# Gate and up projections as seven block products, with the low weight parts taken from PSUM copies

## Chip, cores and metric

One core of one Trainium2 chip. The metric is the device time of the whole kernel in microseconds, the median of several runs; lower is better. Weights and activations are float32.

## What is computed

Three transformer layers over 512 tokens of width 1024: one with a sparse attention and a recurrent branch, then two with differential attention and a pooling branch. The part that matters here stands at the end of each layer (D is 1024, the hidden width 2816):

```python
x = x + merged @ w_out
h2 = rmsnorm(x, norm2_g)
x = x + (silu(h2 @ w_gate) * (h2 @ w_up)) @ w_down
```

## The kernel before

Everything is kept transposed: features on the 128 partitions, the 512 tokens along the columns, so that a [1024, 512] activation is 8 tiles of 128x512 (`xT`). Every float32 matmul is made of three in the fast float32 mode: each operand is split into a high part (rounded) and a low part (the rest), and high x high, high x low and low x high are summed in PSUM. A weight chunk is one column of eight 128x128 tiles (`chunk`, L1058): 24 matmuls of 512 columns for 8 tiles. SyncE loads chunks into a ring of four raw buffers `wraw` (`load`, L530); an engine splits a chunk into a slot (high part first, then low part), and the counters `w_hi` and `w_lo` tell how many chunks are split, `used` how many TensorE has read. `drained` counts result tiles taken out of PSUM.

The end of a layer is the `tail`, written once per engine (L522, L875, L1953, L2664): 8 chunks of w_out; 44 chunks of gate and up in turn; 24 chunks of down, three for each of 8 output tiles (8, 8 and 6 weight tiles). The PSUM banks are `psA` (2), `psS` (2), `psT` (3) and `psO` (1). In the tail:

- GpSimd splits all weights but w_out's first two chunks (`split`, L735: L743 makes the high part, L745 the low part), into two slots, for down into three. It may write a slot when the chunk two (or three) before has been used.
- VectorE adds each w_out tile to `xT` (L1472), makes its low part (L1474) and sums the squares for the norm (L1479); ScalarE makes the high part (L2347) and the square (L2348). After the eighth tile TensorE sums over the partitions (`norm`, L1092) behind the first gate chunk, and ScalarE and VectorE turn that into the scale `c_rs` (L2337 to L2341, L1484 to L1487).
- VectorE drains each gate and up chunk with the scale (L1461), multiplies the two (L1966) and makes the low part (L1969); ScalarE makes the silu (L2672) and the high part (L2674). The result `hid` [2, 22 tiles, 512] is what down reads.
- VectorE adds down's tiles to `xT` and prepares the next layer's operands, as for w_out.

Each engine works its list in order, and only the counters tie the lists together. The matmuls of the second and third layer's query, key and value stage (`rows`, L1307) have 256 columns each.

## Time and profile before

| | us |
|---|---|
| median of 3 runs | 2600.02 (2596.5 to 2602.19) |
| span of the profiled execution | 2597.4 |
| TensorE busy | 2538.9 |
| VectorE busy | 1200.3 |
| ScalarE busy | 834.5 |
| GpSimd busy | 1159.6 |

The page's busy table gives the share of the span for which each engine works; the chain tells which work ended last, step by step, and how much of the span it carries. Rows of a group "line engine op, out<-in" show busy time, the mean duration of one instruction in ns, and the idle time before them with who ended it. Rows of a timeline show start, duration, engine, line and shape, and in brackets the idle time before and who ended it; matmuls one after another are merged into one row with their count.

### The profile page before, as it was taken

The numbers are of one execution on the slowest core, as the hardware profiler recorded it, in microseconds if no ns is written. First come the engines' busy times: TensorE is split into PE (matmuls) and PEld (weight loads), VectorE is DVE, ScalarE is ACT, GpSimd is POOL, SyncE is SP. The second block draws the span as 40 slices with busy tenths as digits, with TensorE's granted clock in tenths as the row PEclk, the third lists the DMA queues.
The fourth block names the chain that finished last, engine by engine and source line by source line (L and its number), as shares of the span: only waits on it lengthen the run. The fifth ranks groups of instructions, "written<-read, shape, count | busy, mean of one in ns | idle before, by whom it ended". The sixth has DMA issues, their size and how long they took to land.

```text
span 2597.4 us, 37755 instructions
## 1 busy us (share of the span) xinstructions
PE 2538.9 (98%) x12947; PEld 2154.6 (83%) x12947; DVE 1200.3 (46%) x2275; ACT 834.5 (32%) x1473; POOL 1159.6 (45%) x586
## 2 busy tenths in 40 slices
PE   7999999999999999999999999999999999999998
PEld 6789988887888888899988888888899888888887
DVE  6567776664432221277775322211577765322211
ACT  4456655663211110144444211100244443211101
POOL 4335530000377788600000777788300002877885
PEclk8989989999999999999999999999999999999999
DMA  7321113332333333322232233333222222333332
GB/s 156 105 49 33 38 37 89 98 90 81 93 92 97 97 101 97 93 70 70 70 94 83 87 93 96 96 103 94 87 82 70 70 82 81 97 97 97 95 95 77
DMA packets 422189, 222.88 MB, mean 86 GB/s; under 512 B 59504, under 2 KB 420268, under 8 KB 422060
## 3 DMA queue, kind: packets, MB, share of 16 engines
q1 hardware_dynamic: 419100, 218.03, 29.6%
q10 hardware_dynamic: 2960, 3.22, 0.4%
q8 instruction: 71, 1.16, 0.2%
q14 instruction: 58, 0.48, 0.1%
HBM read 212.86 MB, written 2.10 MB: 83 GB/s over the span
## 4 chain that ended last, share of the span: by engine, by line
PE 88%; DVE 7%; ACT 3%; issue 2%; DMA 0%; DVEq 0%; ACTq 0%; POOL 0%
PE psA L1066 48%; PE psB L1089 13%; PE psA L1089 10%; PE psA L1322 5%; PE psB L1322 4%; PE psO L967 3%; PE psB L948 1%; PE psB L924 1%; DVE b L2013 1%; DVE b L2161 1%; DVE b L2053 0%; DVE b L1688 0%; DVE b L2034 0%; PE psO L1362 0%; DVE b L1672 0%
## 5 line engine op out<-in xcount | busy, mean ns | idle before, releaser
L1066 PE MATMUL psA<-b,b 128*128 128x512 f32 x5616 | 1288.0, 391 | 3.8 <-DVE b L1461 1.8
L1066 PEld LDWEIGHTS psA<-b,b 128*128 128x128 f32 x5616 | 1055.3, 188 | 234.5 <-issue 8.6
L743 POOL TENSOR_TENSOR b<-b,b 128x1024 fp32r<-128x1024 f32 x239 | 453.0, 1895 | 1202.5 <-PE psA L1066 1042.3
L745 POOL TENSOR_TENSOR b<-b,b 128x1024 fp32r<-128x1024 f32 x239 | 593.9, 2485 | 18.8
L1089 PE MATMUL psB<-b,b 128*128 128x512 f32 (+4 forms) x1626 | 367.3, 384 | 7.7 <-DVE b L1897 4.5
L1089 PEld LDWEIGHTS psB<-b,b 128*128 128x128 f32 (+2 forms) x1626 | 299.1, 195 | 68.1 <-DVE b L1897 4.9
L1089 PE MATMUL psA<-b,b 128*128 128x512 f32 x1356 | 324.4, 394 | 0.0
L1461 DVE SCALAR_TENSOR_TENSOR b<-psA,b 128x512 f32<-128x512 f32 x152 | 104.6, 690 | 461.6 <-PE psA L1066 457.7
L1089 PEld LDWEIGHTS psA<-b,b 128*128 128x128 f32 x1356 | 252.6, 188 | 54.4 <-issue 1.0
L1472 DVE TENSOR_TENSOR b<-b,psA 128x512 f32 x48 | 33.0, 688 | 337.9 <-PE psA L1066 337.9
L2347 ACT ACTIVATE b<-b,b (+1 forms) x56 | 40.6, 724 | 441.1 <-DVE b L1472 434.5
L2674 ACT ACTIVATE b<-psB 128x512 f32 x66 | 39.5, 598 | 370.3 <-DVE psB L1966 370.3
L1322 PE MATMUL psA<-b,b 128*128 128x256 f32 x1152 | 148.7, 288 | 2.2 <-DVE b L1472 2.2
L1322 PE MATMUL psB<-b,b 128*128 128x256 f32 x1152 | 147.8, 288 | 0.5 <-DVE b L2013 0.5
L1322 PEld LDWEIGHTS psA<-b,b 128*128 128x128 f32 x1152 | 143.7, 194 | 5.6 <-issue 4.9
L1322 PEld LDWEIGHTS psB<-b,b 128*128 128x128 f32 x1152 | 143.2, 194 | 2.7 <-issue 2.3
L2013 DVE TENSOR_TENSOR b<-b,b 128x1024 fp32r<-128x1024 f32 x102 | 124.4, 1220 | 13.7 <-ACT b L2689 13.7
L2689 ACT ACTIVATE b<-b 128x1024 fp32r<-128x1024 f32 x102 | 106.3, 1058 | 55.0 <-PE psA L1089 30.6
L2672 ACT ACTIVATE psB<-b 128x512 f32<-128x512 f32 x66 | 39.7, 602 | 251.9 <-DVE b L1461 251.9
L967 PE MATMUL psO<-b,b 128*128 128x128 f32 x640 | 83.3, 287 | 4.8 <-ACT b L2464 2.5
L967 PEld LDWEIGHTS psO<-b,b 128*128 128x128 f32 x640 | 79.5, 202 | 8.1 <-DVE b L1735 3.5
L2457 ACT ACTIVATE b<-b,b 128x512 f32<-128x512 f32 (+3 forms) x128 | 70.3, 551 | 45.1 <-DVE b L1681 45.1
(271 smaller groups left out, 2177.2 us busy)
## 6 DMA issues: line engine op xcount, KB each, us to landing
b<-in_w_in SPq DMA_DIRECT2D x296, 256.0 KB, 3.0
b<-in_w_ffn_in SPq DMA_DIRECT2D x176, 256.0 KB, 3.1
b<-in_w_ffn_out SPq DMA_DIRECT2D x64, 256.0 KB, 3.0
b<-in_w_out SPq DMA_DIRECT2D x48, 256.0 KB, 3.0
b<-in_w_gate SPq DMA_DIRECT2D x44, 256.0 KB, 3.1
b<-in_w_up SPq DMA_DIRECT2D x44, 256.0 KB, 3.2
b<-in_w_down SPq DMA_DIRECT2D x32, 256.0 KB, 3.0
b<-in_w_ffn_out SPq DMA_DIRECT2D x32, 192.0 KB, 2.6
```

The costliest lines, as they stand in the source:

```text
L743: nc.gpsimd.tensor_tensor(w[:, 0], wraw[:, s], ones[:, 0:1].broadcast_to([P, KT * P]), ALU.mult).then_inc(w_hi.sem, 1)
L745: nc.gpsimd.tensor_tensor(w[:, 1], wraw[:, s], hi_f(w[:, 0]), ALU.subtract).then_inc(w_lo.sem, 1)
L967: i = mm(psO[:, qt * P:(qt + 1) * P], PT[:, h, at:at + P], vtok[:, br, kt, n // 4, hd, :, :].rearrange("p h d -> p (h d)"), start=h == 0 a ...
L1066: i = mm(dst, w[:, wh, kt * P:(kt + 1) * P], rhs(xh, kt), start=first and kt == 0 and n == 0, stop=last and kt == kts - 1 and n == 2)
L1089: i = mm(dst, lh(x), rh(y), start=start and n == 0, stop=stop and n == 2, skip_group_check=skip)
L1322: i = mm(ring(t + q // 2)[:, q % 2 * V2:(q % 2 + 1) * V2], xg[:, xh, kt, q * P:(q + 1) * P], w[:, wh, k * V2:(k + 1) * V2], start=kt == 0 ...
L1461: v.scalar_tensor_tensor(dst, psA[:, s % 2, :], -0.5, c_rs[:, :], ALU.mult, ALU.mult).then_inc(drained.sem, 1)
L2013: v.tensor_tensor(w[:, 1], wraw[:, c % RAW], hi_f(w[:, 0]), ALU.subtract).then_inc(w_lo.sem, 1)
L2347: ac(flat(xg)[:, 0, bass.ds(m * T, T)], x, ACT.Copy, scale=gain).then_inc(res_act.sem, 1)
L2457: ac(pq, pq, ACT.Exp, bias=st[:, o + qt:o + 1 + qt], scale=-1.0, accum_out=st[:, o + 8 + qt:o + 9 + qt]).then_inc(ue_act.sem, 1)
L2672: ac(psS[:, 0, :], fg[:, :], ACT.Silu).then_inc(ff_act.sem, 1)
L2689: ac(w[:, 0], wraw[:, c % RAW], ACT.Copy).then_inc(w_hi.sem, 1)
```

## The change

Gate and up of two hidden tiles each (a "quad": 256 hidden columns of gate, 256 of up) were 4 chunks, 96 matmuls of 512 columns. Seen as blocks, the weights are 2x2 (gate or up; even or odd input tiles) and the activations 2x2 (even or odd input tiles; first or second 256 tokens). Now Winograd's form of Strassen's scheme takes seven block products in place of eight: S1 = A21+A22, S2 = S1-A11, S3 = A11-A21, S4 = A12-S2 of the weights (A11 gate even, A12 gate odd, A21 up even, A22 up odd), and t1 to t4 of the activations. One product is 24 matmuls of 256 columns (`product`); there are 11 quads, 77 products a layer, in unrolled code.

- **Loads.** SyncE loads a quad's four raw blocks with four transfers of 512 KB into one of two buffers (`wraw` and the new `wraw2`), the down weights of the first four chunks ahead of time.
- **Sums of weights.** GpSimd makes S1, S2, S4, S3 (`sum_low`, `sum_high`), splits off the low parts of A12 and A22 (`low`), and adds the first and the fifth product. It no longer splits w_out's chunks; down's it still does, from when the last product's weights are ready.
- **Splits.** ScalarE makes the high parts of all seven (`hi`), and for A11, S1, S2, S4 and S3 copies the source to two PSUM banks (`psS`), from which VectorE makes the low part (`lo`). Each slot is one of three. ScalarE and VectorE split w_out's chunks 2 to 7 as well (`out_hi`, `out_lo`, two instructions over 1024 columns a chunk).
- **Operands.** While w_out runs, ScalarE and VectorE make t1 to t4 and the high and low parts for all of them from the tiles of `xT` (`even_operands`, `odd_operands`, `odd_lo`). The norm's matmul comes behind the second product.
- **Results.** VectorE sums the products in PSUM (`middle_sum`, `gate_high`, `gate_low`, `up`: seven instructions a quad of 512 columns), ScalarE makes one silu of 1024 columns a quad, VectorE two products into `hid_raw`. The up half isn't scaled by the norm; down's result is, before it is added.
- **Hidden parts.** `hid` lies over `hid_raw`, the operands and the raw weights, so its parts are made at the end, 11 times over 1024 columns each: ScalarE the high part (`hidden_hi`), VectorE the low part (`hidden_lo`). TensorE's first down column waits for them pair by pair.

The diff, cut to its core:

```diff
-            stage(c0 + 8, 2 * FT, lambda i, s: (up if s % 2 else gate)(i * 2 * P + (s // 2) * P))
-            stage(c0 + 8 + 2 * FT, 24, lambda i, s: down(s % 3 * KT, i * 4 * P + (s // 3) * P), per=12)
...
+            for q in range(QUADS):
+                if q == 0:
+                    mixed()
+                elif q == 1:
+                    sp.wait_ge(w_lo.sem, w_lo.at(c1 - 1))
+                else:
+                    sp.wait_ge(w_lo.sem, w_lo.at(c1 + place_of(q - 2, S3)))
+                settled(sp)
+                for x in range(2):
+                    for b in range(2):
+                        dst = quad_raw(q)[:, 2 * x + b, :].rearrange("p (j n) -> p j n", n=2 * P)
+                        sp.dma_start(dst, quad(x, b, q)).then_inc(quad_in[q % 2], 16)
...
+            sp.wait_ge(w_lo.sem, w_lo.at(c1 + place_of(QUADS - 2, S3)))
+            settled(sp)
+            for s in range(24):
+                load(c2 + s, s % RAW, down(s % 3 * KT, s // 3 * P), free=s < RAW)
...
+                def sum_low(q):
+                    pool.wait_ge(quad_in[q % 2], loads(q))
+                    settled(pool)
+                    if q:
+                        pool.wait_ge(w_lo.sem, w_lo.at(c + place_of(q - 1, S4)))
+                        settled(pool)
+                    raw = quad_raw(q)
+                    nc.gpsimd.tensor_tensor(sum1[:, :], raw[:, 2, :], raw[:, 3, :], ALU.add).then_inc(sa_pool.sem, 1)
+                    pool.wait_ge(sa_pool.sem, sa_pool.at(g + q, "s1"))
+                    settled(pool)
+                    nc.gpsimd.tensor_tensor(sum2[:, :], sum1[:, :], raw[:, 0, :], ALU.subtract).then_inc(sa_pool.sem, 1)
+                def sum_high(q):
+                    raw = quad_raw(q)
+                    pool.wait_ge(sa_pool.sem, sa_pool.at(g + q, "s2"))
+                    settled(pool)
+                    pool.wait_ge(w_lo.sem, w_lo.at(c + place_of(q, S1)))
+                    settled(pool)
+                    nc.gpsimd.tensor_tensor(sum1[:, :], raw[:, 1, :], sum2[:, :], ALU.subtract).then_inc(sa_pool.sem, 1)
+                    nc.gpsimd.tensor_tensor(raw[:, 2, :], raw[:, 0, :], raw[:, 2, :], ALU.subtract).then_inc(sa_pool.sem, 1)
...
+                    if q == 0:
+                        low(q, A12)
+                    sum_high(q)
+                    if q:
+                        low(q, A12)
+                    low(q, A22)
+                    pool.wait_ge(fs_act.sem, fs_act.at(g + q, "fifth"))
+                    settled(pool)
+                    nc.gpsimd.tensor_tensor(fifth_product, fifth_product, first_product, ALU.add).then_inc(ff_pool.sem, 1)
             def down_splits(c, r):
...
+                pool.wait_ge(w_hi.sem, w_hi.at(c - 1))
+                settled(pool)
+                pool.wait_ge(w_lo.sem, w_lo.at(c - 1))
+                settled(pool)
                 with pool.Fori(0, 2) as i:
...
+                            i = nc.tensor.matmul(banks[x][:, p * half_t:(p + 1) * half_t], w[:, wh, at:at + P], rhs[x][:, xh, j, :],
+                                                 start=first and j == 0 and p == 0 and m == 0,
+                                                 stop=last and j == KT // 2 - 1 and p == 1 and m == 2, skip_group_check=True)
+                i.then_inc(used.sem, 1)
...
+                    if x == A11 and q:
+                        pe.wait_ge(fs_dve.sem, fs_dve.at(g + (q - 1), "g1"))
+                    elif x == A11:
+                        pe.wait_ge(drained.sem, drained.at(t0 + 6))
...
+                        if q == 0:
+                            norm(k, n + 7)
+                            pe.wait_ge(xo_dve.sem, xo_dve.at(x0 + 3, "lo_low"))
+                        pe.wait_ge(fs_act.sem, fs_act.at(g + q, "first"))
+                    elif x == A22 and q:
...
+                        if kt % 2 == 0:
+                            pe.wait_ge(fl_dve.sem, fl_dve.at(g + (q * KT + kt) // 2))
...
+                def even_operands(j):
+                    dve.wait_ge(res_act.sem, res_act.at(n + 2 * j, "hi"))
+                    v.tensor_tensor(even2[:, half_t:T], even2[:, T:T + half_t], even2[:, 0:half_t], ALU.subtract).then_inc(xo_dve.sem, 1)
+                    dve.wait_ge(xo_act.sem, xo_act.at(x0 + j, "hi_even"))
+                    dve.wait_ge(xo_dve.sem, xo_dve.at(x0 + j, "t1"))
+                    v.tensor_tensor(xe[:, 1, 0:2, j, :], even2[:, 0:T].rearrange("p (u t) -> p u t", u=2), hi_f(xe[:, 0, 0:2, j, :]), ALU.subtract).then_inc(res_dve.sem, 1)
+                def odd_operands(j):
+                    dve.wait_ge(res_act.sem, res_act.at(n + 2 * j + 1, "hi"))
+                    v.tensor_tensor(odd_high[:, half_t:T], odd_high[:, 0:half_t], even2[:, half_t:T], ALU.subtract).then_inc(xo_dve.sem, 1)
+                    dve.wait_ge(xo_dve.sem, xo_dve.at(x0 + j, "t2"))
+                    dve.wait_ge(xo_act.sem, xo_act.at(x0 + j, "low"))
+                    v.tensor_tensor(odd_high[:, T:T + half_t], odd_high[:, half_t:T], odd_low, ALU.subtract).then_inc(xo_dve.sem, 1)
+                    v.tensor_tensor(odd_high[:, T + half_t:2 * T], odd_high[:, 0:half_t], even2[:, T:T + half_t], ALU.subtract).then_inc(xo_dve.sem, 1)
+                    dve.wait_ge(xo_act.sem, xo_act.at(x0 + j, "hi_low"))
+                    v.tensor_tensor(xe[:, 1, 2, j, :], odd_low, hi_f(xe[:, 0, 2, j, :]), ALU.subtract).then_inc(xo_dve.sem, 1)
+                def odd_lo(j):
+                    dve.wait_ge(xo_act.sem, xo_act.at(x0 + j))
+                    dve.wait_ge(xo_dve.sem, xo_dve.at(x0 + j, "t3"))
+                    v.tensor_tensor(other[:, 1, :, j, :], odd_high.rearrange("p (u t) -> p u t", u=4), hi_f(other[:, 0, :, j, :]), ALU.subtract).then_inc(res_dve.sem, 1)
...
+                    w = quad_slot(at)
+                    v.tensor_tensor(w[:, 1], psS[:, :, :].rearrange("p b t -> p (b t)"), hi_f(w[:, 0]), ALU.subtract).then_inc(w_lo.sem, 1)
...
+                def up(q):
+                    dve.wait_ge(used.sem, used.at(c1 + place_of(q, S3)))
+                    step(v.tensor_tensor(n_r0[:, :], psA[:, 1, :], first_product, ALU.add))
+                    own(q, "u3")
+                    step(v.scalar_tensor_tensor(psT[:, 2, :], psT[:, 2, :], -1.0, n_r0[:, :], ALU.mult, ALU.add))
+                    dve.wait_ge(ff_pool.sem, ff_pool.at(g + q))
+                    step(v.tensor_tensor(psA[:, 1, :], psA[:, 1, :], fifth_product, ALU.add))
...
+                def hidden_lo(i):
+                    dve.wait_ge(fh_act.sem, fh_act.at(g + i))
+                    at = slice(2 * i, 2 * i + 2)
+                    v.tensor_tensor(hid[:, 0, at, :], hid_raw[:, at, :], hi_f(hid[:, 1, 2 * i:2 * i + 2, :]), ALU.subtract).then_inc(fl_dve.sem, 1)
...
+                    dve.wait_ge(used.sem, used.at(c2 + (3 * m + 2)))
+                    v.scalar_tensor_tensor(psA[:, s, :], psA[:, s, :], -0.5, c_rs[:, :], ALU.mult, ALU.mult).then_inc(dn_dve.sem, 1)
+                    dve.wait_ge(dn_dve.sem, dn_dve.at(d0 + m))
+                    v.tensor_tensor(xT[:, m, :], xT[:, m, :], psA[:, s, :], ALU.add).then_inc(drained.sem, 1)
...
+                for j in range(KT // 2):
+                    added(2 * j)
+                    for w in out_ahead.get(2 * j, []):
+                        out_lo(w)
+                    even_operands(j)
+                    squares_added(2 * j)
+                    if j == 3:
+                        lo(0, A11)
+                        lo(0, S1)
+                    added(2 * j + 1)
+                    for w in out_ahead.get(2 * j + 1, []):
+                        out_lo(w)
+                    odd_operands(j)
+                    squares_added(2 * j + 1)
+                    odd_lo(j)
+                lo(0, S2)
+                lo(0, S4)
                 norm(k)
...
+                for q in range(1, QUADS):
+                    up(q - 1)
+                    product_high(q - 1)
+                    lo(q, S2)
+                    product_low(q - 1)
+                    lo(q, S4)
+                    middle_sum(q)
+                    gate_high(q)
+                    lo(q, S3)
+                    gate_low(q)
+                    if q < QUADS - 1:
+                        lo(q + 1, A11)
+                        lo(q + 1, S1)
+                q = QUADS - 1
+                for i in range(4):
+                    hidden_lo(i)
+                up(q)
+                product_high(q)
+                product_low(q)
+                for i in range(4, 6):
+                    hidden_lo(i)
+                for i in range(6, QUADS):
+                    hidden_lo(i)
...
+                        return
+                    if x != A11:
+                        act.wait_ge(w_lo.sem, w_lo.at(c1 + place_of(q, {S1: A11, S2: S1, S4: S2, S3: S4}[x])))
+                    elif q:
+                        act.wait_ge(w_lo.sem, w_lo.at(c1 + place_of(q - 1, S3)))
+                    ac(psS[:, :, :].rearrange("p b t -> p (b t)"), src[:, :], ACT.Copy).then_inc(wc_act.sem, 1)
...
+                    if j == 3:
+                        hi(0)
+                        hi(1)
+                        hi(2)
...
+                for q in range(QUADS):
+                    c = SEVEN * q
+                    if q:
+                        hi(c + 2)
+                    first(q)
+                    hi(c + 3)
+                    fifth(q)
+                    hi(c + 4)
+                    if q == 0:
+                        norm(k)
+                        nc.scalar.preload_act_table_set("silu_and_others")
+                    hi(c + 5)
+                    hi(c + 6)
+                    hi(c + 7)
+                    if q == QUADS - 1:
+                        hidden_hi(0)
+                        hidden_hi(1)
+                    hi(c + 8)
+                    silu(q)
+                hidden_hi(2)
+                hidden_hi(3)
+                hidden_hi(4)
+                hidden_hi(5)
+                for i in range(6, QUADS):
+                    hidden_hi(i)
```

## Rows read from the trace of the kernel before

**Rows 1.** The page: span, busy time (share) and instructions, chain by engine.

```profile
span 2597.4 us, 37755 instructions
PE 2538.9 (98%) x12947; PEld 2154.6 (83%) x12947; DVE 1200.3 (46%) x2275; ACT 834.5 (32%) x1473; POOL 1159.6 (45%) x586
...
PE 88%; DVE 7%; ACT 3%; issue 2%; DMA 0%; DVEq 0%; ACTq 0%; POOL 0%
```

**Rows 2.** Chain in order of time: start us, us, what, count of matmuls.

```profile
735.18 350.08 PE psA L1066 x1536
...
1203.61 2.92 PE psB L1322 x24
...
1278.49 8.64 PE psB L1322 x72
```

**Rows 3.** Timeline of the gate/up loop, first layer.

```profile
898.72 0.69 DVE L1461 SCALAR_TENSOR_TENSOR b<-psA,b 128x512 f32<-128x512 f32 x1 [4.75 <-PE psA L1066]
...
900.36 0.60 ACT L2674 ACTIVATE b<-psB 128x512 f32 x1 [5.75 <-DVE psB L1966]
900.82 2.40 POOL L745 TENSOR_TENSOR b<-b,b 128x1024 fp32r<-128x1024 f32 x1
901.13 0.69 DVE L1969 TENSOR_TENSOR b<-psB,b 128x512 f32 x1 [0.90 <-ACT b L2674]
...
904.16 0.69 DVE L1461 SCALAR_TENSOR_TENSOR b<-psA,b 128x512 f32<-128x512 f32 x1 [2.33 <-PE psA L1066]
```

**Rows 4.** Groups by line and shape, whole span: busy us, mean ns, idle before.

```profile
L743 POOL TENSOR_TENSOR b<-b,b 128x1024 fp32r<-128x1024 f32 x239 | 453.0, 1895 | 1202.5 <-PE psA L1066 1042.3 <-issue 134.0 <-PE psB L1089 14.1
...
L2013 DVE TENSOR_TENSOR b<-b,b 128x1024 fp32r<-128x1024 f32 x102 | 124.4, 1220 | 13.7 <-ACT b L2689 13.7
L2689 ACT ACTIVATE b<-b 128x1024 fp32r<-128x1024 f32 x102 | 106.3, 1058 | 55.0 <-PE psA L1089 30.6 <-PE psB L1089 18.4 <-PE psA L1322 4.5
```

**Rows 5.** Timeline of VectorE and GpSimd near the kernel's start.

```profile
12.53 1.89 POOL L743 TENSOR_TENSOR b<-b,b 128x1024 fp32r<-128x1024 f32 x1 [12.09 <-DMA b<-in_w_in]
...
13.57 1.40 DVE L1474 SCALAR_TENSOR_TENSOR b<-b,b,b 128x512 fp32r<-128x512 f32 x1
...
14.50 2.68 POOL L745 TENSOR_TENSOR b<-b,b 128x1024 fp32r<-128x1024 f32 x1
...
46.11 2.37 POOL L752 TENSOR_TENSOR b<-b,b 128x1024 fp32r<-128x1024 f32 x1 [5.15 <-ACT b L2403]
46.58 2.44 DVE L1526 TENSOR_TENSOR b<-b,b 128x512 fp32r<-128x512 f32 x1 [1.38 <-ACT b L2380]
```

**Rows 6.** Timeline of the passage from w_out to gate and up.

```profile
717.65 0.69 DVE L1472 TENSOR_TENSOR b<-b,psA 128x512 f32 x1 [2.25 <-PE psA L1066]
...
723.11 0.69 DVE L1472 TENSOR_TENSOR b<-b,psA 128x512 f32 x1 [2.28 <-PE psA L1066]
...
725.26 1.28 ACT L2332 ACT_TABLE_LOAD   x1
...
735.18 10.05 PE L1066 MATMUL psA<-b,b 128*128 128x512 f32 x43 [0.43 <-DVE b L1461]
```

**Rows 7.** Timeline of the last down tiles and the next layer's first matmuls.

```profile
1070.25 0.69 DVE L1472 TENSOR_TENSOR b<-b,psA 128x512 f32 x1 [11.88 <-PE psA L1066]
...
1085.41 0.69 DVE L1472 TENSOR_TENSOR b<-b,psA 128x512 f32 x1 [11.87 <-PE psA L1066]
...
1086.26 6.02 PE L1322 MATMUL psA<-b,b 128*128 128x256 f32 x48 [1.02 <-DVE b L1472]
```

**Rows 8.** Timeline of TensorE after a long wait.

```profile
600.28 12.95 PE L1089 MATMUL psB<-b,b 128*128 128x512 f32 x48 [4.52 <-DVE b L1897]
```

**Rows 9.** Busy time by stretch: PE, PEld, DVE, ACT, POOL, granted clock, DMA share, GB/s.

```profile
600.00:604.00 4.00, 3.72 (x9) 2.94 (x10) 0.22 (x1) 1.88 (x3) 0.00 (x0) 0.57 0.34 102
```

**Rows 10.** DMA issues: count, size of one, median us to landing.

```profile
b<-in_x SPq DMA_DIRECT2D x4, 512.0 KB, 6.1
```

More of the change, by code:

```diff
@@ L857, in _ @@
-            down_splits(C_DN, C_DN // RAW)
+                    for d in range(12):
+                        split(c + i * 12 + d, i * 3 + r + d // RAW, d % RAW, slots2[d % 3], 3)
+            quads(C_GU, 0, lambda q: (q // 2 + 1) * 64)
+            down_splits(C_DN, R_DN // RAW)
             with pool.Fori(0, LAYERS) as l:
-                c0, r0 = l * C_LAYER + C_B2, l * (C_LAYER // RAW) + C_B2 // RAW
+                c0, r0 = l * C_LAYER + C_B2, l * (R_LAYER // RAW) + R_B2 // RAW
                 split(c0, r0, 0, slots2[0], 3)
@@ L1475, in residual @@
                                        ALU.mult, ALU.subtract).then_inc(res_dve.sem, 1)
-                if not add and n:
+                if add is False and n:
                     dve.wait_ge(res_dve.sem, res_dve.at(n - 1))
```

358 lines of the change are left out of this document (265 added, 93 removed).

## The prediction, made before the changed kernel ran

> **What bounds the kernel now.** I read the page's busy table and chain first: TensorE is busy for 98% of the span and carries 88% of the chain that ended last, while VectorE and GpSimd are busy for less than half [rows 1]. So time can only come from fewer or shorter matmuls, and every wait that a change puts on TensorE counts in full. Then the chain in order of time, for the pace of the two matmul shapes: one layer's gate, up and down run 1536 matmuls of 512 columns in 350.08 us with no gap; matmuls of 256 columns run 72 in 8.64 us, 120.0 ns each, and 24 alone in 2.92 us [rows 2]. VectorE's drains in the gate/up loop start every 5.44 us, one chunk of 24 matmuls, 226.7 ns each [rows 3]. Half the columns thus cost 53%: about 13 ns of each matmul don't shrink (2 x 120.0 against 226.7).
>
> **Part A, the products.** Removed per layer: 44 chunks x 5.44 = 239.4 us. Added: 7 x 11 = 77 products of 24 matmuls with 256 columns. At 2.88 us each 221.8, at 2.92 us 224.8; between runs of 72 and single ones I take 2.90, so 223.3. Saving **16.1 us a layer** (14.6 to 17.6), not the eighth (30 us) that the count of columns promises. The code is unrolled; the rows of 256 columns stand in unrolled code too, so its fetching is in that price.
>
> The Trainium skill ("TensorE: Matmul & The Clock Gate", Back-to-back issue gap) gives a matmul's spacing as its columns at 2.4 GHz and 2.5 ns. By it the saving would be an estimated 26 us a layer (44 x 24 at 215.8 ns less 77 x 24 at 109.2). The rows show about 13 ns in place of 2.5 [rows 2, 3], and the sum goes by the rows.
>
> **Do the helpers keep up in the steady quads?** A quad lasts 7 x 2.9 = 20.3 us of TensorE. ScalarE: 12 passes over 1024 columns (7 high parts, 5 PSUM copies; 1.06 each), a silu of 1024 (about 1.1) and 2 copies of 512 (0.60): 15.0 us. VectorE: 5 low parts at 1.22 and 9 sums or products at 0.69: 12.3 us. GpSimd: 6 passes of 2.40 and one of 512 (half, plus overhead, 1.3): 15.7 us [rows 3, 4]. All below 20.3. The tightest chain, with 0.15 us per hand-over, counted from the start of a quad: `up` of the quad before starts at 0.75 (behind the low part of S1), three sums end at 2.95, the product at 3.75, the low part of S2 at 4.95; TensorE wants S2 at 5.8. Its copy then lets S4 be ready at 7.5 (wanted 8.7); GpSimd's A12 is ready at 10.35 (11.6), A22 at 12.85 (14.5). Behind S4's copy, which waits for S2's low part, ScalarE has `fifth` and A12's high part in its queue, and GpSimd's A12 hangs on them: that is in the 10.35. Slack 0.85 us or more: zero cost. If the cover were gone by 1 us per quad, it would be 33 us in all. SyncE issues the loads of 2 MB a quad about 19 us before GpSimd wants them; 512 KB pieces landed within 6.1 us (median) [rows 10].
>
> **The port.** Now where VectorE works on two SBUF operands while GpSimd runs. GpSimd L752 runs 46.11 to 48.48; VectorE's L1526 starts in it at 46.58 and takes 2.44 instead of the 0.69 of such 512-column work, ending 0.54 after it. Between 12.5 and 17.2 they take turns: L1474, 1.40 long, ends 0.55 after L743, and L745 behind it takes 2.68 instead of 2.40 [rows 5]. So one waits for the other's whole instruction. Where one VectorE operand is in PSUM, neither is hurt: L1969 inside L745 takes 0.69, and L745 its 2.40 [rows 3]. The steady quads' VectorE work all has a PSUM operand, so that is where the PSUM copies pay. Not so the operand preparation ahead of quad 0 and the hidden low parts after quad 10. The Trainium skill ("SBUF — State Buffer", Who interferes with whom) says that two SBUF inputs contend with GpSimd's reads as an exclusive lock for a whole instruction; the trace agrees (2.44 for 0.69).
>
> **Part B, the start.** Chunks 6 and 7 of w_out end at 717.5 and 722.95 [rows 6]. While w_out runs, VectorE now also does six weight low parts (1.22) and the operands: a pair of tiles has about 8 us of its own work plus up to two low parts, against 10.9 of TensorE. Quad 0's weights arrive near 702 (SyncE waits for chunk 3's low part at 692.8, then 5 transfers), and GpSimd's two sums put 2.4 us each in VectorE's way. I get tile 6 added at 721.7 instead of 717.7. From there: add 0.7, scale 0.7, difference, high, low of the even operands, squares (to 726.0, hand-overs in), ScalarE's high part of A11 and its copy to 726.65, low part to 728.1: **A11 starts 5.2 us late**, with 0.35 of waiting earlier. Then the low part of S1 at 730.6, tile 7 added 731.3, ScalarE's scalings 732.2. VectorE's t2 waits for GpSimd's A12 (to 733.15), GpSimd's S4 sum follows (735.9), t4, GpSimd's S3 sum (738.6), t3, low, squares, ScalarE's high part, odd low part at 741.5. S1's product ended at 734.0, so **the norm waits 7.5 us**. Behind it ScalarE has first, two high parts with copies, fifth, a high part, a table load (1.28), the roots (2.0), another load and A22's high part, and GpSimd 2.4: A22 at 753.7, **2.9 us late**. Sum 15.9, less what the old start loses (0.43 of wait and the drain's lag, 1.3 in all): **14.6 us** a layer. Without the port in it: idles of 1.8, 2.2 and 2.7, less 1.3: about 5.4. To the other side a long idle also meets a slow clock: after 4.52 us idle the granted clock was 0.57 over the next 4 us, mostly the 1.2 GHz level, and 48 matmuls took 12.95 us instead of the 10.9 of rows 3's pace [rows 8, 9]. Most of that falls into the next wait; 1.7 may be left. Range 5 to 17.
>
> **Part C, the end.** From the start of quad 10: GpSimd's down splits wait for S3's low part, 15.2; each is 1.89 + 2.40 [rows 3, 4]. VectorE's 11 low parts of the hidden pairs (1024 columns, two SBUF operands, 1.22, or 1.1 after a wait) begin at 15.8. TensorE ends S3 at 20.2 and then wants a pair every 1.37 us, the last by about 34. Taking turns: low parts 0 to 3 end at 18.3, 21.8, 24.8, 28.3; then `up` and the products (PSUM, 3.6 us); 4 and 5 end at 33.8 and 36.8; GpSimd's third and fourth split push the last to 45 to 47. TensorE ends the first column at 48 instead of 35.3: 13. If VectorE instead keeps the port through a run, GpSimd's first split is ready at 24.3 instead of 20.7, the second at 36.9 and the third at 41.2, and the column ends at 46.4: 11. The bare port time (11 x 1.15 + 3 x 4.3 from 15.3) gives 41 and 7 us. With something for the clock after the last idle I take **12.5** (7 to 15; 0.3 if the port didn't block).
>
> **Part D.** The down result is scaled before it is added: one more 0.69 and a hand-over on the path to the next stage, where TensorE waits 1.02 for L1472 now [rows 7]: **0.8**. Inside the down loop 15.2 us lie between two drains [rows 7]: nothing.
>
> **The sum.** Per layer -16.1 + 14.6 + 12.5 + 0.8 = +11.8; three layers +35.4. The span of 2597.4 becomes 2632.8; the median of the runs, 2600.0, lies 2.6 above that span [rows 1], so 2635.4.
>
> **The rivals.**
> 1. The port costs next to nothing in these two places (VectorE slips between GpSimd's instructions, or the instructions don't meet). For it: most of VectorE's work here has a PSUM operand. Against it stand both places of [rows 5]. -16.1 + 5.4 + 0.3 + 0.8 = -9.6 a layer: **2571**, faster. It decides by whether L1526's 2.44 repeats in the hidden low parts.
> 2. The port blocks, but the start has the slack that my walk denies it and the end costs its bare port time: -16.1 + 8 + 7 + 0.8 = -0.3: **2599**, no change. For it: my walk chains some thirty steps at 0.15 each.
> 3. The start is mostly covered, the end is not: -16.1 + 7 + 12.5 + 0.8 = +4.2: **2613**.
> 4. The steady chain isn't covered (hand-overs of 0.25 instead of 0.15 eat the 0.85), 1 us a quad on top of the forecast: **2668**. Against: the forecast's chain has few hand-overs between `up` and S2.
> 5. (No case of its own.) The 256-column rate doesn't hold over 20 us at a stretch or the counts don't fall as written: 2.92 and more gives +3.5 us a layer: inside the range.
>
> **How the numbers follow.** Chances: forecast 0.48, rival 1 0.16, rival 2 0.14, rival 3 0.12, rival 4 0.10. A difference of 0.2% (5.2 us) is about what a measurement of this kernel can tell from no change. Faster: rival 1 and half of rival 2's lower side, 0.22. Same: the rest of rival 2 and a little of rival 3, 0.13. Slower: 0.65. The range for 8 in 10 runs from 2566, below rival 1, to 2658; above the worst ends together (starts of 17, ends of 15, products of 2.92: 2655); left out are rival 4 and what no case covers.
>
> **What would show it.** Right: in the gate/up stretch TensorE without idle, groups of 256 columns at 2.88 to 2.92 us per 24; the hidden low parts with a mean of 2 us or more and TensorE waiting for them under L1066 in each of the three layers; a wait of several us ahead of the norm's matmul; split instructions of GpSimd longer than 2.40 in the same places. Wrong: idle inside the quads put down to GpSimd or ScalarE (rival 4), hidden low parts at 1.22 and the down stage starting without a gap (rival 1), or less than 2 us ahead of A11 and of the norm (rivals 2 and 3). If the pace per product is far from 2.9, Part A is wrong.

## The result and the profile after

The changed kernel takes **2615.0 us** (median of 4 runs, 2610.8 to 2620.3) against 2598.8 us of the kernel before in the same runs (2596.5 to 2602.2): a ratio of **1.0062** (95% interval 1.0042 to 1.0081), 16 us slower. The forecast was 35 us slower, 2635. The sign is right and the size is less than half; 2615 lies close to the time of rival 3.

The page of the changed kernel: span, busy table and chain by engine.

```profile
span 2612.9 us, 42576 instructions
...
PE 2503.3 (96%) x15323; PEld 2231.3 (85%) x15323; DVE 1577.8 (60%) x2608; ACT 1289.9 (49%) x1935; POOL 1044.2 (40%) x517
...
PE 81%; DVE 12%; ACT 4%; issue 3%; POOL 0%; DMA 0%; ACTq 0%; DVEq 0%; POOLq 0%
```

TensorE's busy time falls by 35.6 us against [rows 1], and the span grows by 15.5: 51 us of waiting are new. Its share of the chain falls from 88% to 81%, VectorE's rises from 7% to 12%. The waits of the changed kernel name the places (TensorE's longest totals; us, times, longest):

```profile
PE psA L1212 <- DVE b L2201: 23.7, 16, 3.7
PE psO L1240 <- DVE b L2133: 15.4, 3, 5.3
...
PE psA L990 <- DVE b L2147: 10.1, 3, 3.6
```

L1212 is the down projection waiting for the hidden tiles' low parts, L1240 the norm's matmul waiting for the last right operand, L990 the first product of each layer's quads waiting for its weights' low part. There are three layers, and none of these waits lies in the steady quads. TensorE's timeline there (start us, us, count of matmuls; a wait of TensorE would stand in brackets):

```profile
804.35 2.98 PE L990 MATMUL psA<-b,b 128*128 128x256 f32 x24
807.17 3.04 PE L990 MATMUL psB<-b,b 128*128 128x256 f32 x24
810.05 3.04 PE L990 MATMUL psA<-b,b 128*128 128x256 f32 x24
812.93 2.98 PE L990 MATMUL psB<-b,b 128*128 128x256 f32 x24
815.74 5.92 PE L990 MATMUL psA<-b,b 128*128 128x256 f32 x48
821.50 2.98 PE L990 MATMUL psB<-b,b 128*128 128x256 f32 x24
824.31 3.04 PE L990 MATMUL psA<-b,b 128*128 128x256 f32 x24
```

From 804.35 to 824.31 lie seven products, 2.85 us each. From 749.89 to the last product's start at 955.79 there are 72 without a wait: 2.860 us a product, 119.2 ns a matmul.

The start of the quads and the end, same view, with one row of GpSimd (the low part of A22's weights) and the first matmul of A22 behind it at 752.81:

```profile
728.44 4.61 PE L990 MATMUL psA<-b,b 128*128 128x256 f32 x24 [2.98 <-DVE b L2147]
732.89 3.04 PE L990 MATMUL psB<-b,b 128*128 128x256 f32 x24
740.94 2.08 PE L1240 MATMUL psO<-b,b 128*128 128x512 f32 x2 [5.01 <-DVE b L2133]
742.03 8.03 PE L990 MATMUL psA<-b,b 128*128 128x256 f32 x48
...
750.33 2.42 POOL L936 TENSOR_TENSOR b<-b,b 128x1024 fp32r<-128x1024 f32 x1 [12.08 <-ACT b L3000]
...
752.81 0.38 PE L990 MATMUL psB<-b,b 128*128 128x256 f32 x1
...
959.53 3.04 PE L1212 MATMUL psA<-b,b 128*128 128x512 f32 x12 [0.70 <-issue]
...
966.73 1.67 PE L1212 MATMUL psA<-b,b 128*128 128x512 f32 x6 [1.66 <-DVE b L2201]
972.08 5.67 PE L1212 MATMUL psA<-b,b 128*128 128x512 f32 x12 [3.68 <-DVE b L2201]
```

Besides the waits, matmuls behind them are slow: 24 in 4.61 us instead of 3.0, 48 in 8.03 instead of 5.9, 12 in 5.67 instead of 3.0. The granted clock from 726 to 752 is about 0.8, where the kernel before has 1.00 from 728 to 735; from 972 to 978 it is 0.50. Whether slow matmuls cost time depends on what comes next. A22 has no wait in brackets (in the third layer one of 0.26), yet its first matmul starts 0.06 us after GpSimd's low part lands at 752.75, and in the two later layers 0.05 us after it. So TensorE, slowed as it was, arrived there just as its operand did.

What stretches the two chains, in the timeline of VectorE and GpSimd:

```profile
730.85 2.38 POOL L936 TENSOR_TENSOR b<-b,b 128x1024 fp32r<-128x1024 f32 x1 [20.05 <-DVE b L2147]
732.24 1.28 DVE L2122 TENSOR_TENSOR b<-b,b 128x256 f32<-128x256 f32 x1 [0.97 <-ACT b L2976]
733.20 2.58 POOL L926 TENSOR_TENSOR b<-b,b 128x1024 f32<-128x1024 f32 x1
733.55 2.50 DVE L2125 TENSOR_TENSOR b<-b,b 128x256 f32<-128x256 f32 x1
735.73 2.52 POOL L927 TENSOR_TENSOR b<-b 128x1024 f32<-128x1024 f32 x1
735.98 2.56 DVE L2126 TENSOR_TENSOR b<-b,b 128x256 f32<-128x256 f32 x1
...
954.19 1.90 POOL L803 TENSOR_TENSOR b<-b,b 128x1024 fp32r<-128x1024 f32 x1 [1.58 <-DVE b L2147]
954.21 12.46 DVE L2201 TENSOR_TENSOR b<-b,b 128x1024 fp32r<-128x1024 f32 x4
956.17 3.26 POOL L805 TENSOR_TENSOR b<-b,b 128x1024 fp32r<-128x1024 f32 x1
959.39 2.88 POOL L803 TENSOR_TENSOR b<-b,b 128x1024 fp32r<-128x1024 f32 x1
```

Each of VectorE's steps on two SBUF operands ends a fraction of a us after a step of GpSimd, and each GpSimd step behind one of them is longer than it is alone: the pattern of [rows 5], now on TensorE's path. A 256-column difference takes 2.5 us instead of the 0.42 that it takes elsewhere in this trace; the first four hidden low parts take 12.46 us, 3.1 each.

### The profile page after: what moved, and what is told of

Same layout as the page of the kernel before. It is cut to its first block, busy times and chain, and to the rows that moved or that the text cites. A ratio compares the mean times of both kernels' runs of the same rounds, so it can differ in the third digit from the quotient of the medians.

```text
span 2612.9 us, 42576 instructions
## 1 busy us (share of the span) xinstructions
PE 2503.3 (96%) x15323; PEld 2231.3 (85%) x15323; DVE 1577.8 (60%) x2608; ACT 1289.9 (49%) x1935; POOL 1044.2 (40%) x517
## 4 chain that ended last, share of the span: by engine, by line
PE 81%; DVE 12%; ACT 4%; issue 3%; POOL 0%; DMA 0%; ACTq 0%; DVEq 0%; POOLq 0%
PE psA L1212 16%; PE psA L990 14%; PE psB L1235 13%; PE psB L990 10%; PE psA L1235 10%; PE psA L1468 5%; PE psB L1468 4%; DVE b L2201 3%; PE psO L1113 3%; PE psB L1094 2%; PE psB L1070 1%; DVE b L2126 1%; DVE b L2302 1%; DVE b L2450 0%; DVE b L2323 0%
## 5 line engine op out<-in xcount | busy, mean ns | idle before, releaser
L1212 PE MATMUL psA<-b,b 128*128 128x512 f32 x2448 | 577.8, 397 | 28.0 <-DVE b L2201 23.7
L1212 PEld LDWEIGHTS psA<-b,b 128*128 128x128 f32 x2448 | 462.2, 190 | 141.3 <-DVE b L2201 19.9
L915 POOL TENSOR_TENSOR b<-b 128x1024 f32<-128x1024 f32 x33 | 80.0, 2423 | 1030.5 <-DMA b<-in_w_ffn_in 725.1
L990 PE MATMUL psA<-b,b 128*128 128x256 f32 x3168 | 404.0, 286 | 10.1 <-DVE b L2147 10.1
L990 PEld LDWEIGHTS psA<-b,b 128*128 128x128 f32 x3168 | 393.0, 194 | 14.5 <-DVE b L2147 8.0
L1235 PE MATMUL psA<-b,b 128*128 128x512 f32 x1356 | 324.4, 394 | 0.0
L3000 ACT ACTIVATE b<-b 128x1024 fp32r<-128x1024 f32 x231 | 244.2, 1057 | 148.3 <-PE psB L990 79.1
L990 PE MATMUL psB<-b,b 128*128 128x256 f32 x2376 | 299.2, 282 | 0.3 <-POOL b L936 0.3
L1235 PEld LDWEIGHTS psA<-b,b 128*128 128x128 f32 x1356 | 252.5, 188 | 54.4 <-issue 1.0
L990 PEld LDWEIGHTS psB<-b,b 128*128 128x128 f32 x2376 | 290.0, 191 | 0.8 <-POOL b L936 0.7
L2147 DVE TENSOR_TENSOR b<-psB,b 128x1024 fp32r<-128x1024 f32 x165 | 201.8, 1223 | 128.0 <-ACT psB L3007 121.0
L805 POOL TENSOR_TENSOR b<-b,b 128x1024 fp32r<-128x1024 f32 x89 | 235.6, 2647 | 7.0
L936 POOL TENSOR_TENSOR b<-b,b 128x1024 fp32r<-128x1024 f32 x66 | 159.2, 2413 | 166.3 <-ACT b L3000 100.0
L803 POOL TENSOR_TENSOR b<-b,b 128x1024 fp32r<-128x1024 f32 x89 | 178.1, 2001 | 87.8 <-PE psA L1212 36.0
L3007 ACT ACTIVATE psB<-b 128x1024 f32<-128x1024 f32 x165 | 167.2, 1013 | 1.9 <-DVE b L2147 1.5
L1468 PE MATMUL psA<-b,b 128*128 128x256 f32 x1152 | 148.6, 288 | 3.2 <-DVE b L2208 3.2
L1468 PEld LDWEIGHTS psA<-b,b 128*128 128x128 f32 x1152 | 143.6, 194 | 6.7 <-issue 6.0
L1468 PE MATMUL psB<-b,b 128*128 128x256 f32 x1152 | 144.8, 284 | 0.5 <-DVE b L2302 0.5
```

The lines of the kernel that those rows point to most:

```text
L803: nc.gpsimd.tensor_tensor(w[:, 0], wraw[:, s], ones[:, 0:1].broadcast_to([P, KT * P]), ALU.mult).then_inc(w_hi.sem, 1)
L805: nc.gpsimd.tensor_tensor(w[:, 1], wraw[:, s], hi_f(w[:, 0]), ALU.subtract).then_inc(w_lo.sem, 1)
L915: nc.gpsimd.tensor_tensor(sum1[:, :], raw[:, 2, :], raw[:, 3, :], ALU.add).then_inc(sa_pool.sem, 1)
L936: nc.gpsimd.tensor_tensor(w[:, 1], quad_raw(q)[:, {A12: 1, A22: 3}[x]], hi_f(w[:, 0]), ALU.subtract).then_inc(w_lo.sem, 1)
L990: i = nc.tensor.matmul(banks[x][:, p * half_t:(p + 1) * half_t], w[:, wh, at:at + P], rhs[x][:, xh, j, :], start=first and j == 0 and p == ...
L1212: i = mm(dst, w[:, wh, kt * P:(kt + 1) * P], rhs(xh, kt), start=first and kt == 0 and n == 0, stop=last and kt == kts - 1 and n == 2)
```

## The experiments

The theory: the losses at the two ends come from VectorE and GpSimd taking turns at SBUF, each for a whole instruction; the gain is the products' count at the price of a narrow matmul. The rivals: the chains of weights, sums and norm are late by themselves; TensorE's clock is the cost; the narrow matmul costs something else than the forecast says. The first three runs leave out the right values of the steps that they change (the PSUM bank holds other numbers), so they tell the time alone; the others compute the whole result.

**The end without the turns.**

```diff
-  v.tensor_tensor(hid[:, 0, at, :], hid_raw[:, at, :], hi_f(...), ALU.subtract)
+  v.tensor_tensor(hid[:, 0, at, :], psS[:, :, :], hi_f(...), ALU.subtract)
```

> The changed kernel, in which the low part of each pair of hidden tiles (L2201) subtracts from 1024 values of a PSUM bank in place of the tiles in SBUF; so the right low parts of the hidden tiles are left out, and nothing else differs: same count, same shapes, same waits. Port theory: VectorE and GpSimd take turns at the SBUF port between 954 and 984 us of each layer's trace; without the turns VectorE's eleven subtractions take 11 x 1.22 = 13.5 us instead of the 26.9 us (12.46 + 14.41) in the trace, GpSimd's pairs 4.4 us instead of 6.1, and the down projection loses about 1 us instead of 12.0: 3 x 11 = 33 us less than 2615, about 2582. Rival: the end waits for the weights' own split on GpSimd and for the last product's chain, which this edit doesn't touch: 0 to 6 us less, 2609 to 2615.

Measured: 2578.5 us (ratio to the kernel before 0.992, 0.9903 to 0.9938), 36.5 less than the changed kernel. By shape, the hidden low parts of the changed kernel and of this one (count, busy us, mean ns):

```profile
L2201 DVE TENSOR_TENSOR b<-b,b 128x1024 fp32r<-128x1024 f32 x33 | 80.8, 2510 | 0.1
```

```profile
L2201 DVE TENSOR_TENSOR b<-psB,b 128x1024 fp32r<-128x1024 f32 x33 | 38.1, 1214 | 1.6 <-ACT b L3031 1.5
```

TensorE's down projection starts without a gap and takes 121.5 us a layer instead of 133.4, and GpSimd makes the same splits. So where the subtraction reads its second operand is worth 11.9 us a layer; the weights' split was not late by itself.

**The start without the turns.**

```diff
-  v.tensor_tensor(odd_high[:, T:T + half_t], odd_high[:, half_t:T], odd_low, ALU.subtract)
+  v.tensor_tensor(odd_high[:, T:T + half_t], psO[:, 0:half_t], odd_low, ALU.subtract)
...
```

> The changed kernel, in which seven of VectorE's operations on two SBUF operands in the w_out stage (the four differences of the right operands and the three low parts, L2115 to L2133) take one operand from a PSUM bank of the same size; the right differences and low parts are left out, counts, shapes and waits are the same. Port theory of the start: GpSimd's L936, L926 and L927 (2.38, 2.58, 2.52 us) stretch L2122, L2125 and L2126 to 1.28, 2.50 and 2.56 us instead of 0.43 each; without that the wait ahead of the norm's matmul falls from 5.0 to about 1 us, the clock may fall less, and the first product starts as before. 4 to 5 us per layer, 12 to 15 us in all: about 2601. Rival (ScalarE's chain of copies bounds the start as well): no more than 1 us per layer, 2612 to 2615.

Measured: 2593.4 us (0.9979, 0.997 to 0.9989), 21.6 less than the changed kernel, 7.2 a layer, more than the 4 to 5 expected. TensorE at this kernel's start of the quads:

```profile
720.82 3.10 PE L990 MATMUL psA<-b,b 128*128 128x256 f32 x24 [0.31 <-DVE b L2147]
...
728.24 1.13 PE L1240 MATMUL psO<-b,b 128*128 128x512 f32 x2 [1.44 <-DVE b L2133]
728.80 6.28 PE L990 MATMUL psA<-b,b 128*128 128x256 f32 x48
...
740.03 3.11 PE L990 MATMUL psB<-b,b 128*128 128x256 f32 x24 [2.08 <-POOL b L936]
```

The wait ahead of A11 went too, from 2.98 to 0.31: GpSimd's two sums at 705.8 (L915, L918) had stretched VectorE's L2125 and L2126 of the second operand pair to 2.60 and 2.65 us, and no other turns ahead of A11 go with this edit. What I had missed is that turns 20 us ahead of a wait still count when the chain between has no slack: VectorE idles there for 0.2 to 1 us at a time, but mostly for a step of ScalarE on VectorE's own last result. In the later layers the wait ahead of A11 fell from 3.6 to about 1. The granted clock stays at 1.00 from 720 to 752. A wait of 2.08 us now shows at A22, but it is no new loss: A22's low part lands 11.7 us after the norm's matmul starts (728.24 to 739.98), in the changed kernel 11.8 (740.94 to 752.75). There the slow matmuls covered the same delay.

**Both.** 

> The changed kernel with both PSUM substitutions of the earlier runs (hidden low parts at the end, seven operand steps in the w_out stage); the right values of those low parts and differences are left out. It gives the time without the port's turns at either end. If the two losses are apart from each other, the gains add: against 2615, 36.5 us from the end (2615.0 - 2578.5) and 21.6 from the start (2615.0 - 2593.4) make 2557. Rival (one wait hides behind the other): 2565 to 2575.

Measured: 2560.1 us (0.986, 0.9841 to 0.9879), 54.9 less than the changed kernel against 58.1 for the sum, and the runs lie between 2554.7 and 2565.6: within that scatter the two losses add.

**The steady quads without the PSUM copies.**

```diff
-  dve.wait_ge(wc_act.sem, wc_act.at(g + q, ...))
-  v.tensor_tensor(w[:, 1], psS[:, :, :].rearrange("p b t -> p (b t)"), hi_f(w[:, 0]), ALU.subtract)
+  v.tensor_tensor(w[:, 1], src[:, :], hi_f(w[:, 0]), ALU.subtract)    # src: the weights or the sum in SBUF
...
-  ac(psS[:, :, :].rearrange("p b t -> p (b t)"), src[:, :], ACT.Copy).then_inc(wc_act.sem, 1)
```

> The changed kernel without its PSUM copies: VectorE's low parts of the weights (L2147) read the weights and sums in SBUF, and ScalarE's copies (L3007, 1.01 us, five per quad) are gone; the result is whole. Port theory of the steady quads: per quad GpSimd holds the port for six operations of 2.4 us and one of 1.28 (15.8 us), VectorE's five low parts need 5 x 1.22 = 6.1 us of it, together 21.9 us against the 20.03 us that TensorE takes: at least 1.9 us more per quad, 33 quads, 62 us, and more where turns fall badly: 2670 to 2760. Rival (the copies were not needed, ScalarE's relief is worth as much): 2605 to 2620.

Measured: 2693.8 us (1.036, 1.0341 to 1.0378), 79 more than the changed kernel. The low parts of the weights take 2.29 us instead of 1.22, and TensorE waits for them 31 times; this kernel's low parts, its largest wait, and the changed kernel's low parts:

```profile
L2148 DVE TENSOR_TENSOR b<-b,b 128x1024 fp32r<-128x1024 f32 x165 | 378.3, 2293 | 15.8 <-ACT b L3001 12.6 <-POOL b L936 0.7
```

```profile
PE psA L990 <- DVE b L2148: 57.8, 31, 3.0
```

```profile
L2147 DVE TENSOR_TENSOR b<-psB,b 128x1024 fp32r<-128x1024 f32 x165 | 201.8, 1223 | 128.0 <-ACT psB L3007 121.0 <-POOL b L936 6.4 <-issue 0.6
```

GpSimd's two first sums of a quad stretch too (L915 from 2.42 to 3.32 us, L918 from 2.41 to 3.10). So the copies are what lets the quads run without a gap: ScalarE spends 1.01 us on each of 165 and they are worth 79 us.

**The narrow matmul by itself.** In the kernel before:

```diff
-  i = mm(dst, w[:, wh, kt * P:(kt + 1) * P], rhs(xh, kt), ...)
+  for p in range(2):                      # two matmuls of 256 columns
+      at = slice(p * T // 2, (p + 1) * T // 2)
+      i = nc.tensor.matmul(psA[:, s % 2, at], w[:, wh, kt * P:(kt + 1) * P], rhs(xh, kt)[:, at], ...)
```

> The kernel before, in which each 512-column matmul of gate and up is issued as two of 256 columns (48 instead of 24 per chunk, 44 chunks in each of three layers); the result is whole. It measures the price of a narrow matmul by itself. By the changed kernel's steady quads, 20.03 us for 7 x 24 matmuls = 119.2 ns each against 226.7 ns for one of 512: 48 x 0.1192 = 5.72 against 5.44 us per chunk, 0.28 x 132 = 37 us more, about 2636. By the price that the prediction used (2.90 us for 24, 120.8 ns): 5.80 against 5.44, 47 us more, 2646. Rival (half the columns, half the time; the loss of the changed kernel lies elsewhere): 2600.

Measured: 2639.7 us (1.0152, 1.0134 to 1.017), 40.4 more, 0.306 us a chunk: (5.44 + 0.306) / 48 = 119.7 ns. That confirms the pace of the quads (119.2) within 0.5% and lies below the 120.8 ns (2.90 us for 24) that the prediction took.

**Moving the work at the end.** ScalarE and VectorE split the first four chunks of down between the hidden halves; GpSimd starts at chunk 4:

```diff
+  pool.wait_ge(fl_dve.sem, fl_dve.at(g + QUADS - 1))
...
-  with pool.Fori(0, 2) as i:
-      for d in range(12):
-          split(c + i * 12 + d, ...)
+  for d in range(4, 24):
+      split(c + d, r + d // RAW, d % RAW, slots2[d % 3], 3)
```

> The changed kernel, in which the first four chunks of the down projection's weights are split by ScalarE (high) and VectorE (low), woven in between the hidden tiles' halves, and GpSimd starts at chunk 4 once the last hidden low part is done; the result is whole. It tells whether the port can be kept apart by moving work. Port theory: the end loses what VectorE's own queue then costs: from the last quad's gate on it has 11 x 1.22 + 3 x 1.22 + 3.4 us of the last quad's steps = 20.5 us of work from 954.2 on, done at 974.7, where TensorE would want the last pair at 972.5, so 2 to 4 us lost instead of 12.0: 3 x 9 = 27 us less than 2615, about 2588 (2582 to 2594). Rival (the weights' splits were late by themselves, whoever makes them): 2605 to 2615.

Measured: 2583.8 us (0.9949, 0.9933 to 0.9966), 31 less than the changed kernel. One wait is left at the end of each layer:

```profile
956.01 11.26 PE L1215 MATMUL psA<-b,b 128*128 128x512 f32 x48
969.41 20.90 PE L1215 MATMUL psA<-b,b 128*128 128x512 f32 x90 [2.14 <-DVE b L2204]
```

It is 2.14 us (2.02 in the later layers), inside the 2 to 4 that the expectation worked out from VectorE's own queue; down takes 123.7 us a layer instead of 133.4.

**Moving the sums at the start.**

```diff
+  if q == 0:
+      pool.wait_ge(res_dve.sem, res_dve.at(n + 7))     # ahead of L926 and L927
```

> The changed kernel, in which GpSimd's sums of the first quad's S4 and S3 (L926, L927) also wait until the last right operand's low part is made; the result is whole. Port theory: L2125 and L2126 of the last operand pair take 0.43 us instead of 2.50 and 2.56, so the norm's matmul starts 3 to 4 us earlier, if the S4 sum, which is then finished near 739 us instead of 735.8, stays hidden behind S1, A12 and S2: 3 x 3.5 = 10 us less than 2615, 2600 to 2606. Rival (the sum becomes late: S4 waits for it): 2612 to 2618.

Measured: 2611.9 us (1.0052, 1.0036 to 1.0069), only 3.1 less. Neither the theory's size nor the rival's place is right:

```profile
725.25 4.60 PE L993 MATMUL psA<-b,b 128*128 128x256 f32 x24 [3.03 <-DVE b L2150]
...
733.52 1.13 PE L1243 MATMUL psO<-b,b 128*128 128x512 f32 x2 [0.79 <-DVE b L2136]
734.08 6.29 PE L993 MATMUL psA<-b,b 128*128 128x256 f32 x48
...
746.72 4.59 PE L993 MATMUL psB<-b,b 128*128 128x256 f32 x24 [3.47 <-POOL b L939]
```

The norm's wait fell from 5.01 to 0.79 as expected, and 3.47 us show at A22. The norm's matmul starts 4.2 us sooner after w_out's end, but A22's low part only 2.9 (24.4 us after it instead of 27.3), and over the whole layer 1.5 us are left. That low part GpSimd can't make before ScalarE has made the high part, and the high part stands in ScalarE's queue behind the norm's table load and steps. S4, which the rival named, waits for nothing. The next run moves it.

```diff
-  if q == 0:
-      norm(k)
-      nc.scalar.preload_act_table_set("silu_and_others")
   hi(c + 5)                                            # A22's high part
+  if q == 0:
+      norm(k)
+      nc.scalar.preload_act_table_set("silu_and_others")
```

> The kernel with GpSimd's later sums after the operands, and besides A12 ahead of the norm's matmul on TensorE and ScalarE's split of A22's weights ahead of the norm's steps; the result is whole. In the run without the order (2611.9) the wait for the norm's matmul fell from 5.01 to 0.79 us, but TensorE then waited 3.47 us for A22's low part (L936), whose high part stood on ScalarE behind the norm's table load and three steps. Theory (the wait moved there): with the order the 3.5 us come out, less some 1 us for A12's own wait on t3: 3 x 2.5 = 7.5 us less than 2611.9, 2602 to 2606. Rival (GpSimd itself is late with A22 because its sums were put back): 2609 to 2613.

Measured: 2607.4 us (1.0035, 1.0021 to 1.0049), 4.5 less than without the order, less than the 7.5 of the theory and more than the rival allows: A22's wait is gone, but a wait of 1.67 us stands at the first product behind it, for its weights' low part on VectorE, and in the two later layers that wait is 3.41.

**The clock.** In the changed kernel, matmuls without use in the two waits at the start:

```diff
+  for i in range(16):                                  # 32 ahead of the norm's wait
+      nc.tensor.matmul(psO[:, 0:half_t], src[:, 0, 0, 0:P], src[:, 0, 1, 0:half_t], start=True, stop=True)
```

> The changed kernel with matmuls of no use in TensorE's two waits at the start of the quads: 16 of 256 columns (about 1.9 us) ahead of the first product's wait of 2.98 us, 32 (3.8 us) ahead of the norm's wait of 5.01 us; the result is whole. Granted clock between 726 and 752 us is 0.79 to 0.81 in the changed kernel against 1.00 in the same place of the kernel before. Clock theory: TensorE's idle time lowers the clock, which costs 1.6 us in A11 (4.61 against 3.0), 1.0 in the norm's matmul, 1 to 2 us in the 48 matmuls after: 3 to 4 us per layer, so 2604 to 2606. Rival (the stretched matmuls have another cause, or the filler delays the real work): 2614 to 2620.

Measured: 2616.7 us (1.0071, 1.005 to 1.0093): the rival's number. The stretches in question (us; PE, PEld, DVE, ACT and POOL busy; granted clock; DMA share; GB/s), changed kernel, then this one:

```profile
726.00:735.00 9.00, 6.56 (x42) 6.59 (x43) 6.21 (x6) 5.67 (x9) 4.15 (x2) 0.81 0.01 3
735.00:742.00 7.00, 1.99 (x10) 1.27 (x10) 5.69 (x5) 3.43 (x5) 3.25 (x2) 0.79 0.00 0
742.00:752.00 10.00, 10.00 (x68) 9.48 (x67) 5.01 (x6) 9.78 (x11) 1.67 (x1) 0.81 0.00 0
```

```profile
726.00:735.00 9.00, 7.97 (x58) 7.38 (x57) 4.86 (x7) 7.66 (x11) 1.49 (x1) 1.00 0.00 1
735.00:742.00 7.00, 5.93 (x50) 5.72 (x48) 6.96 (x5) 1.33 (x3) 6.01 (x3) 1.00 0.00 0
742.00:752.00 10.00, 8.30 (x53) 7.27 (x54) 5.34 (x7) 9.88 (x13) 0.00 (x0) 0.83 0.01 2
```

The filler holds the clock at its full level, 2.4 GHz, up to 742, and A11 takes 3.11 us again. But the norm's matmul starts 15.7 us after w_out's end, in the changed kernel 15.5: VectorE sets that moment, and A11's slow matmuls lay inside the wait. Behind the norm 2.77 us of idle time were left uncovered and the matmul there took 2.08 us as before; 0.9 us gained in the 48 matmuls after it went into a wait of 0.75 at A22. A lower clock inside a stretch that waits anyway costs nothing. Behind the norm this run didn't remove it, but the traces settle that part too: A22 starts when its low part lands, in this run (755.48, start at 755.53) as in the changed kernel (752.75, 752.81), and GpSimd's low part waits for ScalarE (L3000), not for TensorE. So up to A22 none of the loss is the clock's.

**All moves together.** The kernel v3 has both moves, the new order, and A11's weights one operand pair earlier.

> The changed kernel with the edits of the two runs beside it (the first four chunks of down split by ScalarE and VectorE; the first quad's later sums after the operands), and with a new order at the start of the quads: the weights of the first product are split one operand pair earlier, A12 runs ahead of the norm's matmul, ScalarE splits A22's weights ahead of the norm's steps. The result is whole. Port and order theory: 27 us from the end, 10 us from the sums, and 1 to 3 us per layer from the A11 and norm waits and the clock that falls with them: 2615 - 27 - 10 - 6 = 2572 (2564 to 2582), below the kernel before at 2599. Rival (ends gain, start is bounded by ScalarE's own chain): 2580 to 2588.

Measured: 2575.5 us (0.991, 0.9893 to 0.9927), inside the theory's range. The kernel v4 adds four moves, the first from a line of v3's trace in the second layer: the norm's scale on VectorE, two SBUF operands, met GpSimd's sums for the second quad, and S3 waited (VectorE, then TensorE):

```profile
1486.04 2.94 DVE L1637 SCALAR_TENSOR_TENSOR b<-b,b 128x512 f32<-128x512 f32 x1
...
1491.65 6.20 PE L996 MATMUL psA<-b,b 128*128 128x256 f32 x48 [3.41 <-DVE b L2152]
```

```diff
+  if q == 1:
+      pool.wait_ge(nm_dve.sem, nm_dve.at(k, "scale"))  # ahead of the second quad's sums
...
+  pool.wait_ge(fl_dve.sem, fl_dve.at(g + 8))           # VectorE is now in five steps that read PSUM
+  nc.gpsimd.tensor_tensor(slots2[2][:, 1], wraw[:, 2], hi_f(slots2[2][:, 0]), ALU.subtract)
```

> The kernel of v3_both_ends with four more moves, the result whole: GpSimd's sums for the second quad wait until VectorE has the norm's scale (in layers 2 and 3 L915 and L918 stretched L1637 to 2.94 us and S3 waited 3.41 us); ScalarE loads silu's table after S3's weights; at the end GpSimd makes the low part of chunk 2 while VectorE is in the five steps of the last quad that read PSUM; these five steps stand ahead of pair 9 instead of pair 8. Port theory: start 2 us less in each of layers 2 and 3, end 2.14 us of wait become 1.1 in each of three layers: 4 + 3 = 7 us less than 2575.5, 2566 to 2571. Rival (GpSimd's step beside PSUM reads is not free, or its later sums are late for S1 and S2 of the second quad): 2574 to 2580.

Measured: **2559.1 us** (0.9845, 0.9828 to 0.9861), 16 less than v3 and 9 less than the theory's middle. Between the two traces the three layers give 14.8 of it: 1.8 a layer in the stretch from w_out's end to the last product, 3.1 in down (125.3 to 122.2). The four moves weren't run one by one, so how much each brings is not shown. In its trace the scale takes 0.69 again and S3's wait is 1.18. At the end GpSimd's low part and VectorE's steps run side by side, and neither is stretched:

```profile
1695.84 0.68 DVE L2197 TENSOR_TENSOR b<-psA,b 128x512 f32<-128x512 f32 x1
1696.10 2.40 POOL L966 TENSOR_TENSOR b<-b,b 128x1024 fp32r<-128x1024 f32 x1 [14.90 <-ACT b L3057]
1696.56 0.70 DVE L2199 SCALAR_TENSOR_TENSOR psB<-psB,b 128x512 f32<-128x512 f32 x1
```

Down takes 122.2 us a layer, 0.8 above the run without turns. Per layer, from w_out's end to the last product, the stretch is 226.1 us on average (changed kernel 233.9, v3 227.9). It is 1.5% faster than the kernel before and 2.1% faster than the changed one.

## Why the prediction was half right

Per layer the changed kernel takes, from w_out's start to down's end, 411.0 us (681.18 to 1092.16). In the kernel before, w_out starts at 679.15 and down ends at 1085.24 [rows 7]: 406.1. So 4.9 a layer (5.2 and 5.3 in the later two), and 0.6 behind it; the forecast had 11.8. The mechanism held: the losses came where the forecast put them and by the turns that it named. Two terms of its sum were mis-sized, the price of a product in Part A and the walk up to the norm in Part B.

- **A, the products: forecast -16.1, measured -19.2** (77 x 2.860 = 220.2 against 239.4). The step that failed is "between runs of 72 and single ones I take 2.90". [rows 2] offered 120.0 ns a matmul over a run of 72 and 121.7 over 24 alone. The longest run, 2.88 us a product, would have taken away 1.5 of the error of 3.1 us a layer; that the pace over 72 products is 2.860 no row of before showed. That half the columns cost 53% of the time was right, and it is why the count's eighth didn't come: measured 119.7 ns against 226.7 for twice the columns, 12.7 ns a matmul that don't shrink.
- **B, the start: forecast +14.6, measured about +12.2** (4.9 + 19.2 - 11.9, the last being C). The step that failed is the walk up to the norm's matmul. It put that matmul 18.5 us after w_out's end (A11 5.2 late, two products of 2.9, a wait of 7.5); measured are 15.5, with waits of 2.98 and 5.01 for the same releasers and 1.6 us of slow clock in A11 between them, which the norm's wait would have held otherwise. Already tile 6 was added 2.9 us later than in the kernel before (41.4 against 38.5 us after w_out's start), where the walk had 4.0. "A22 2.9 us late" was nearly right: A22 starts 11.9 us after the norm's matmul, forecast 12.2. It shows as slow matmuls (2.08 and 8.03 us for work of 1.0 and 5.9) in place of a wait. So the clock at nothing, "most of that falls into the next wait", was right as well. The port's part is 7.2 a layer (second run), forecast 14.6 - 5.4 = 9.2; what remains without it is 5.0, forecast 5.4.
- **C, the end: forecast +12.5, measured +11.9** (133.4 against 121.5 in the first run). Mechanism, place and size as forecast: VectorE and GpSimd alternate through the stretch, the hidden low parts average 2.51 us ("2 us or more"), and the last one ends 45.7 us after the last quad's start (938.65 to 984.32), where the walk had 45 to 47. The 12 matmuls at half the clock (5.67 us) end ahead of further waits for low parts.
- **D: forecast +0.8, measured +0.6** (the wait ahead of the next layer's first matmul is 1.62 against 1.02).
- **Steady quads: zero cost, right.** No wait of TensorE lies there; rival 4 is out. The run without PSUM copies shows how little room there was: 79 us hung on them.
- **Rivals.** Rival 1 (the port costs nothing) falls with the first two runs, 36.5 and 21.6 us. Rival 2 had the end at 7, measured are 11.9. Rival 3 gave 2613 by a start of +7 and no error in A; its time is the measured one, its reason is not: the start cost 12.2 and A brought 3.1 more.

The sum of the measured terms is -19.2 + 12.2 + 11.9 + 0.6 = +5.5 a layer, 16.5 in all, against 16.1 between the medians. That fit is partly luck: the part from the end of down to the next w_out takes 343.1 us instead of 344.3, although it holds D's 0.6, and w_out starts 2.0 later in the first layer; neither is explained. Of the 6.3 us a layer between forecast and result, A's price makes 3.1 and B's walk 2.4. The sum was a small difference of large terms (16, 15 and 13), so errors of a fifth in two of them halved it; the range, 2566 to 2658, held.

Not explained: w_out's start in the first layer lies between 676.2 and 687.0 us in these kernels, although the runs' edits leave the code ahead of it as it is; such differences of single executions are why the terms were taken between two points of one trace.

## What to carry to other kernels

When a change shifts work to VectorE or GpSimd, list for every stretch which instructions of the two have two SBUF inputs; where they meet, add the other's whole instruction to each, and look for turns long ahead of the wait that they end in. Three remedies are shown here: a PSUM source for one operand (79 us hung on it in the quads), GpSimd's work given to ScalarE and to VectorE's own queue while GpSimd waits (31), and waits that move GpSimd's work beside PSUM-reading steps (16, together with two other moves). After a fix follow the queue of each engine to the next wait: behind the norm's wait stood one at A22, which slow matmuls had covered, and behind that one at the next product.

A reduction in the count of matmuls is worth its columns less a fixed part for each instruction (12.7 ns here); take the price from the longest unbroken run of that shape.
